# TensorE takes the attention steps of a two-layer hybrid encoder in pairs

## The reference, cut to what matters

```
h   = RMSNorm(x);  q, k, v, g of three mixers = h @ w_in
A   : 12 heads, windowed (+-128 tokens), sink logit, relative bias
B   : 12 heads, dense, normed and rotated q/k
C   : 8 heads, three dilated groups, merged by their softmax denominators
x   = x + concat(A*silu(gA), B*silu(gB), C*silu(gC)) @ w_out
```

## Time and profile before

| | |
|---|---|
| median of 3 runs | 2954.18 us (2950.13 to 2955.64) |
| the profiled execution | 2959.1 us, its span 2957.3 us |
| PE busy | 2899.2 us, 98% of the span |
| DVE, ACT, POOL busy | 1318.9, 1144.8, 921.4 us |
| mean granted TensorE clock | 0.985 of full speed |

### The profile page before, as it was taken

The page is one execution under the profiler, slowest core; times in us unless marked ns, Lnnn a source line. Parts: engine busy times, 40 slices in busy tenths (PEclk is TensorE's granted clock), DMA queues, the critical chain, the costliest instruction groups (busy, mean ns, idle before and its releaser), DMA issues. The chain is left out here.

```text
span 2957.3 us, 43364 instructions
## 1 busy us (share of the span) xinstructions
PE 2899.2 (98%) x15201; PEld 2572.9 (87%) x15201; DVE 1318.9 (45%) x3437; ACT 1144.8 (39%) x2841; POOL 921.4 (31%) x838
## 2 busy tenths in 40 slices
PE   8999999999999999999999999999999999999999
PEld 6888899989999999888888888999899998998887
DVE  3334433325776567522322344333347755774221
ACT  4322223326665466422322322222356644663111
POOL 0233322210663477200002333323006634771000
PEclk9999999998999999999999999999979999999999
DMA  4334333467445332433323343334764453324332
GB/s 165 84 104 111 103 111 100 108 165 200 123 115 129 110 94 72 152 123 102 100 86 91 104 118 107 100 100 109 187 177 106 113 133 99 103 69 164 107 100 93
DMA packets 382034, 342.74 MB, mean 116 GB/s; under 512 B 60055, under 2 KB 310071, under 8 KB 381820
## 3 DMA queue, kind: packets, MB, share of 16 engines
q1 hardware_dynamic: 381820, 339.98, 40.1%
HBM read 256.03 MB, written 83.86 MB: 115 GB/s over the span
## 5 line engine op out<-in xcount | busy, mean ns | idle before, releaser
L1244 PE MATMUL bank<-w_hi,act_hi 128*128 128x512 f32 x2496 | 1001.1, 401 | 4.7 <-DVE w_lo L1667 4.7
L1245 PE MATMUL bank<-w_lo,act_hi 128*128 128x512 f32 x2496 | 989.4, 396 | 0.0
L1246 PE MATMUL bank<-w_hi,act_lo 128*128 128x512 f32 x2496 | 989.1, 396 | 0.0
L1667 DVE TENSOR_TENSOR w_lo<-w_raw,w_hi 128x512 fp32r<-128x512 f32 x544 | 396.2, 730 | 660.9 <-ACT w_hi L1421 659.2
L1421 ACT CAST w_hi<-w_raw 128x512 fp32r<-128x512 f32 x544 | 335.6, 618 | 779.3 <-PE bank L1246 776.9
L1244 PEld LDWEIGHTS bank<-w_hi,act_hi 128*128 128x128 f32 x2496 | 518.2, 208 | 95.8 <-DVE w_lo L1667 5.5
L1246 PEld LDWEIGHTS bank<-w_hi,act_lo 128*128 128x128 f32 x2496 | 518.1, 208 | 95.1
L1245 PEld LDWEIGHTS bank<-w_lo,act_hi 128*128 128x128 f32 x2496 | 518.4, 208 | 88.8
L2024 POOL TENSOR_SCALAR prob<-prob,denom 128x256 f32<-128x256 f32 (+2 forms) x288 | 344.1, 1200 | 322.0 <-DVE denom L1798 321.7
L1267 PE MATMUL bank<-act_hi,w_hi 128*128 128x384 f32 x1024 | 350.4, 342 | 0.0
L1269 PE MATMUL bank<-act_hi,w_lo 128*128 128x384 f32 x1024 | 347.3, 339 | 0.0
(11 more groups left out here) (101 smaller groups left out, 3454.8 us busy)
## 6 DMA issues: line engine op xcount, KB each, us to landing
w_raw<-w_in SPq DMA_DIRECT2D x144, 512.0 KB, 4.1
w_raw<-w_out SPq DMA_DIRECT2D x64, 512.0 KB, 4.4
heads_t<-turned SPq DMA_DIRECT2D x240, 128.0 KB, 2.4
q_t<-heads_t SPq DMA_DIRECT2D x192, 128.0 KB, 2.1
k_t<-keys_t SPq DMA_DIRECT2D x48, 384.0 KB, 5.7
w_raw<-w_in SPq DMA_DIRECT2D x32, 448.0 KB, 3.6
quad_t<-heads_t SPq DMA_DIRECT2D x48, 256.0 KB, 4.8
mix_rows<-mixed_t SPq DMA_DIRECT2D x32, 384.0 KB, 2.7
```

The costliest lines, as they stand in the source:

```text
L1244: pe.matmul(acc[t][:], hi, w_hi[:, n % W_RING, :], start=(k == 0), stop=False)
L1245: pe.matmul(acc[t][:], hi, w_lo[:, n % W_RING, :], start=False, stop=False)
L1246: last = pe.matmul(acc[t][:], lo, w_hi[:, n % W_RING, :], start=False, stop=(k == KC - 1))
L1667: nc.vector.tensor_tensor(w_lo[:, n % W_RING, :], w_raw[:, load % W_RAW, j, :], w_hi[:, n % W_RING, :].bitcast(F32), ALU.subtract).then_in ...
```

## The change

TensorE's list in the loop goes by `PE_TURNS`: the 24 turns of Q one at a time, all later ones in pairs (i, i+1), with i even. For a pair it issues both scores, then the gate pieces of both turns, then what `pair_pv`, the transposes, `pv` and `mix_turn` have for both. The lists of the other engines keep their order turn by turn, as do all lags and the numbers of banks and slots.

Beside it, kind Q's products go to two banks in turn. C's merge is divided: VectorE scales and adds the first three token tiles of the stored parts (`merge_first`), GpSimd the other three (`merge_back`), VectorE's own part comes at turns 6 and 7 after the merge's end where it was 7 and 8, and the transposes at 8 and 10 where they were 9 and 10. `gate_product` works by halves of 384 tokens, one turn apart.

```diff
@@ -307,8 +307,9 @@
 PARTS_TURN = 3
-OWN_TURN = 7
-MIX_TURN = 9
+FRONT_TURN = 4
+OWN_TURN = 6
+MIX_TURNS = (8, 10)
 assert N_PAIRS % STAT_SLOTS == 0 and STAT_SLOTS % TT == 0 and (N_PAIRS - N_MERGES) // 2 % TT == 0
@@ -407,14 +408,26 @@
+def mix_turns(i):
+
+    return [(mc, g) for mc, end in enumerate(MERGE_END) for g, since in enumerate(MIX_TURNS) if i - end == since]
+
+
+
+FIRST_PAIR = next(i for i, x in enumerate(STEPS) if x["kind"] != "Q")
+assert FIRST_PAIR % 2 == N_LOOP % 2 == 0
+PE_TURNS = [(i,) for i in range(FIRST_PAIR)] + [(i, i + 1) for i in range(FIRST_PAIR, N_LOOP, 2)]
+
+
 def bank_users():
     users = []
-    for i in range(N_LOOP):
+    for turns in PE_TURNS:
         for lag, kinds in ((PAIR_LAG, "AB"), (V_LAG, "C")):
-            if 0 <= i - lag < N_STEPS and STEPS[i - lag]["last"] and STEPS[i - lag]["kind"] in kinds:
-                users.append((STEPS[i - lag]["kind"], STEPS[i - lag]["item"]))
-        users += [("mix", (mc, g)) for mc, g in merge_turns(i, MIX_TURN, len(MIX_GROUPS))]
+            for i in turns:
+                if 0 <= i - lag < N_STEPS and STEPS[i - lag]["last"] and STEPS[i - lag]["kind"] in kinds:
+                    users.append((STEPS[i - lag]["kind"], STEPS[i - lag]["item"]))
+        users += [("mix", x) for i in turns for x in mix_turns(i)]
     return users
@@ -471,10 +484,10 @@
 CHUNK_LAST = [max(x["step"] for x in ITEMS if x["kind"] != "Q" and CHUNK_ORDER.index(x["unit"]["chunk"] + x["hp"]) == n) for n in range(KC)]
-PRODUCT_TURN = [max(SILU_TURN[n], CHUNK_LAST[n] + (X_LAG if n in TURNED_CHUNKS else MIX_TURN + len(MIX_GROUPS) - 1)) + 1
+PRODUCT_TURN = [max(SILU_TURN[n], CHUNK_LAST[n] + (X_LAG if n in TURNED_CHUNKS else MIX_TURNS[-1])) + 1
                 for n in range(GATE_TILES)]
-PRODUCT_AT = at_turns(enumerate(PRODUCT_TURN))
-assert all(PRODUCT_TURN[n] < min(i for i, x in GATE_DRAIN_AT.items() if (n + GATE_SLOTS, 0) in x) for n in range(GATE_TILES - GATE_SLOTS))
+PRODUCT_AT = at_turns(((n, h), turn + h) for n, turn in enumerate(PRODUCT_TURN) for h in range(2))
+assert all(PRODUCT_TURN[n] + 1 < min(i for i, x in GATE_DRAIN_AT.items() if (n + GATE_SLOTS, 0) in x) for n in range(GATE_TILES - GATE_SLOTS))
@@ -712,6 +725,7 @@
         merge_parts = sem("merge_parts")
+        merge_front = sem("merge_front")
         kept = sem("kept")
@@ -1036,7 +1050,7 @@
                 at = l * KC + n
-                sp.wait_ge(gated, at + 1)
+                sp.wait_ge(gated, 2 * (at + 1))
                 sp.dma_start(mix_rows[n], mixed_t[:, at % MIX_SLOTS, :]).then_inc(mix_stored[at % MIX_SLOTS], 16)
@@ -1321,9 +1335,10 @@
                 else:
-                    o = o_bank[0]
-                    if it >= 1:
-                        pe.wait_ge(part_taken, l * N_QUADS + ITEMS[it]["quad_no"])
+                    q = ITEMS[it]["quad_no"]
+                    o = o_bank[q % 2]
+                    if q >= 2:
+                        pe.wait_ge(part_taken, l * N_QUADS + q - 1)
                 kv, times = kv_place(l, st["u"])
@@ -1386,20 +1401,25 @@
                 pe.wait_ge(acc_copied, (l + 1) * NS_IN * TT)
-                for i in range(N_LOOP):
-                    first, end = PIECES_BY[i - 1] if i else PIECES_FIRST, PIECES_BY[i]
-                    if i < N_STEPS:
-                        scores(l, i)
-                    for p in range(first, end):
+                for turns in PE_TURNS:
+                    for i in turns:
+                        if i < N_STEPS:
+                            scores(l, i)
+                    first = PIECES_BY[turns[0] - 1] if turns[0] else PIECES_FIRST
+                    for p in range(first, PIECES_BY[turns[-1]]):
                         gate_piece(l, p)
-                    if ends_pair(i - PAIR_LAG):
-                        pair_pv(l, i - PAIR_LAG)
-                    if 0 <= i - T_LAG < N_STEPS:
-                        p_turn(l, i - T_LAG)
-                    if 0 <= i - V_LAG < N_STEPS and not features_first(STEPS[i - V_LAG]):
-                        pv(l, i - V_LAG)
-                    for mc, g in merge_turns(i, MIX_TURN, len(MIX_GROUPS)):
-                        mix_turn(l, mc, g)
+                    for i in turns:
+                        if ends_pair(i - PAIR_LAG):
+                            pair_pv(l, i - PAIR_LAG)
+                    for i in turns:
+                        if 0 <= i - T_LAG < N_STEPS:
+                            p_turn(l, i - T_LAG)
+                    for i in turns:
+                        if 0 <= i - V_LAG < N_STEPS and not features_first(STEPS[i - V_LAG]):
+                            pv(l, i - V_LAG)
+                    for i in turns:
+                        for mc, g in mix_turns(i):
+                            mix_turn(l, mc, g)
@@ -1520,7 +1540,8 @@
                 if ATT_UNITS[u]["kind"] == "B" and ATT_UNITS[u - 1]["kind"] == "C":
-                    act.wait_ge(merge_parts, 3 * (l + 1) * MERGES)
+                    act.wait_ge(merge_parts, 2 * (l + 1) * MERGES)
+                    act.wait_ge(merge_front, 2 * (l + 1) * MERGES)
                 if k > 0:
@@ -1825,7 +1846,7 @@
                 nc.vector.tensor_copy(part_out[:, q % PART_SLOTS, :, 0:2 * DH],
-                                      o_bank[0][:, 0:4 * DH].rearrange("p (h n) -> p h n", h=2)).then_inc(part_taken, 1)
+                                      o_bank[ITEMS[it]["quad_no"] % 2][:, 0:4 * DH].rearrange("p (h n) -> p h n", h=2)).then_inc(part_taken, 1)
@@ -1865,6 +1886,19 @@
+            def merge_first(l, mc):
+
+                m = l * MERGES + mc
+                views = [x[:, 0:TT // 2, :] for x in part_heads]
+                dve.wait_ge(merge_chain, 5 * m + 5)
+                for g in range(2):
+                    v = views[g].rearrange("p t (r d) -> p t r d", d=DH)
+                    w = merge_w[:, g * TT:g * TT + TT // 2, :].unsqueeze(3).broadcast_to([P, TT // 2, 2, DH])
+                    ins = nc.vector.tensor_tensor(v, v, w, ALU.mult)
+                ins.then_inc(merge_front, 1)
+                dve.wait_ge(merge_front, 2 * m + 1)
+                nc.vector.tensor_tensor(views[0], views[0], views[1], ALU.add).then_inc(merge_front, 1)
+
             def merge_own(l, mc, h):
@@ -1875,7 +1909,7 @@
                 dve.wait_ge(merge_scaled, 2 * m + h + 1)
-                dve.wait_ge(merge_parts, 3 * m + 3)
+                dve.wait_ge(merge_parts if h else merge_front, 2 * m + 2)
                 nc.vector.tensor_tensor(own, own, part_heads[0][:, tiles, :], ALU.add).then_inc(merged, 1)
@@ -1884,7 +1918,7 @@
                 if at >= GATE_SLOTS:
-                    dve.wait_ge(gated, at - GATE_SLOTS + 1)
+                    dve.wait_ge(gated, 2 * (at - GATE_SLOTS + 1))
                 tokens = slice(h * HALF, (h + 1) * HALF)
@@ -1949,6 +1983,8 @@
                         merge_weights(l, mc)
+                    for mc, _ in merge_turns(i, FRONT_TURN):
+                        merge_first(l, mc)
                     for mc, h in merge_turns(i, OWN_TURN, 2):
@@ -2033,31 +2069,31 @@
-            def gate_product(l, n):
+            def gate_product(l, n, h):
                 at = l * GATE_TILES + n
-                pool.wait_ge(gate_done, 2 * (at + 1))
+                pool.wait_ge(gate_done, 2 * at + h + 1)
+                tokens = slice(h * HALF, (h + 1) * HALF)
                 if n in TURNED_CHUNKS:
                     pool.wait_ge(mixed, l * N_TURNED + TT * (TURNED_CHUNKS.index(n) + 1))
                 else:
                     pool.wait_ge(mix_copied, (l * MERGES + n + 1 - sum(c < n for c in TURNED_CHUNKS)) * len(MIX_GROUPS))
-                v = mixed_t[:, at % MIX_SLOTS, :]
-                nc.gpsimd.tensor_tensor(v, v, gate_t[:, at % GATE_SLOTS, :], ALU.mult).then_inc(gated, 1)
-
-            def merge_others(l, mc, stage):
+                v = mixed_t[:, at % MIX_SLOTS, tokens]
+                nc.gpsimd.tensor_tensor(v, v, gate_t[:, at % GATE_SLOTS, tokens], ALU.mult).then_inc(gated, 1)
+
+            def merge_back(l, mc, stage):
                 m = l * MERGES + mc
-                pool.wait_ge(merge_chain, 5 * m + 5)
-                if stage < 2:
+                views = [x[:, TT // 2:TT, :] for x in part_heads]
+                if stage == 0:
+                    pool.wait_ge(merge_chain, 5 * m + 5)
                     for g in range(2):
-                        tiles = slice(stage * TT // 2, (stage + 1) * TT // 2)
-                        v = part_heads[g][:, tiles, :].rearrange("p t (r d) -> p t r d", d=DH)
-                        w = merge_w[:, g * TT + stage * TT // 2:g * TT + (stage + 1) * TT // 2, :].unsqueeze(3)
-                        ins = nc.gpsimd.tensor_tensor(v, v, w.broadcast_to([P, TT // 2, 2, DH]), ALU.mult)
+                        v = views[g].rearrange("p t (r d) -> p t r d", d=DH)
+                        w = merge_w[:, g * TT + TT // 2:(g + 1) * TT, :].unsqueeze(3).broadcast_to([P, TT // 2, 2, DH])
```

(14 more changed lines are left out.)

## The result

The changed kernel takes 3315.78 us (median of 4 runs, 3312.74 to 3317.54) against 2953.46 before (median of 4); the ratio is 1.1227, 95% interval 1.1207 to 1.1246. Its profiled span is 3310.9 us, 353.6 more. It is slower by 12.3% where 11.6% was forecast.

A forecast was written before the change was run, and what follows sets the result against it. TensorE's own list was taken to set the pace. Waits 257, splits and drains 70, C's product 5 and clock 61, less gains of 50, gave +343 us and 3297 us against the runs; range 3160 to 3481.

The forecast's parts named there:

- The chain: In A and B pairs, scores wait for copies, exponentials and minimum behind the transposes of i-3: 257 us together.
- Rival 3: Faster: the second step's minimum reaches DVE ahead of the transposes of i-3, nobody waits, 2904 us; chance 0.04.
- The splits: In A and B, 44 odd-turn weight splits between exponential and inversion add 1.25 us each: 55 us.
- The drains: In A and B, 28 even-turn gate drains between low part and inversion add 0.55 us each: 15 us.
- the scores are no trouble: In C, scores were to wait for nothing: DVE has no low part to wait for, two products lie between.
- The product of i-3: In C, this product follows its own transposes in the same pair and waits 0.15 us over 32 pairs: 5 us.
- The clock: Falls of TensorE's clock after waits, taken for three in four of B's 48 four-tile pairs: 61 us.
- The gains: Savings of 50 us in sum, among them 21 of four waits removed and 10 of clock falls after them.
- The 18.5 us for fewer changes between transposes and scores: Gain on TensorE: 0.08 us for 144 pairs, 11.5 us, and in C 0.15 for 48 pairs, 7 us.

The follow-up runs named there:

- e6: The changed kernel with each weight split that falls on an odd turn moved one turn on, 29 a layer: 3217.47 us.
- e3: The changed kernel with the second step's minimum moved ahead of the low part of step i-3 in VectorE's list, TensorE's untouched: 3153.62 us.
- e4: As e3, and on ScalarE both exponentials of a pair also moved ahead of the high copies of i-3 and i-2 respectively: 3060.62 us.
- e2: The changed kernel, pairs kept, with products and transposes ahead of the gate pieces within a pair: 2959.64 us, ratio 1.0014 to before.
- e5: The changed kernel with only the first of a pair's transposes (step i-3) moved ahead of the gate pieces: 3023.73 us.
- e1: The changed kernel with all turns single, its quad banks, divided merge and half products kept: 2924.03 us, ratio 0.9895 to before.

## Why the prediction was right

**The chain.** It holds step by step. To count each wait in full I take from TensorE's timeline the distance between the start of the instruction ahead of the scores and that of the scores, less the same distance where nothing waits. The profile's idle time is shorter, as it begins when the modelled end of the instruction ahead is reached. The first four rows are the usual wait of pairs without a split or drain in the chain, the next two what these add. Changed kernel, us:

| | forecast | measured |
|---|---|---|
| A, second scores, 2 / 3 tiles | 1.31 / a little more | 1.48 / 1.51 |
| B, 4 tiles, first | 1.20 | 1.25 |
| B, 4 tiles, second | 1.13 | 1.06 |
| B, 2 tiles, both together | 2.0 | 2.1 |
| a split on an odd turn adds | 1.25 | 1.1 (A), 1.0 (B), 1.4 (C), by e6 |
| a drain on an even turn adds | 0.55 | 0.2 to 0.3 |
| A, all waits | 132 us | 127 us |
| B, all waits | 195 us | 178 us |
| C, all waits | 0 | 25 us |
| sum | 327 us | 330 us |

e3 and e4 show that the order in DVE's and ACT's lists makes the waits; e2 and e5 show that the transposes' place in TensorE's does; e1 shows that there are none without pairs. Rival 3 named the same point of decision, and the runs put it on the side of the forecast. B's waits are smaller than said: 17 us less in sum, though its usual pair is as forecast.

**The splits.** e6 bears out the term, 1.07 us each by the idle times. The drains were charged at their full 0.55 us and cost about half of that or less. What the prediction missed is C. There it said "the scores are no trouble", because no low part stands ahead of the minimum. But a split does. The pair at 1020 of the changed kernel, on TensorE:

```profile
1020.50 0.36 PE L1310 MATMUL bank<-k_t,q_t 128*128 128x256 f32 x1
...
1022.12 0.39 PE L1310 MATMUL bank<-k_t,q_t 128*128 128x256 f32 x1 [1.14 <-DVE minus_max L1801]
```

On ScalarE:

```profile
1020.26 0.60 ACT L1441 CAST w_hi<-w_raw 128x512 fp32r<-128x512 f32 x1
```

On VectorE:

```profile
1020.90 0.69 DVE L1688 TENSOR_TENSOR w_lo<-w_raw,w_hi 128x512 fp32r<-128x512 f32 x1 [4.24 <-ACT w_hi L1441]
1021.51 0.55 DVE L1801 CUSTOM_DVE_ANT_0 prob<-bank,bias 128x384 f32<-128x384 f32 x1
```

The high part of the weights waits on ScalarE behind the copy of i-3 and the exponential, the low part on VectorE for it, and the minimum of the second step for that. Six of C's pairs a layer wait for such a split (the seventh split stands before a score of B), and three at the start of the stage wait without one while A's last steps are still turned. Together they make 25 us. e6 takes C back to 117.9 us. The product of i-3, priced at 5 us, shows no wait.

**The clock.** Forecast 61 us, all of it in B. By the record of the clock, B stood at 1.2 GHz for 92.2 us in both layers and A for 30.8, which cost at most 46 and 15, 61 in all. The size is right, the place not quite. In A the eight falls all stand at an idle stretch of 1.9 to 3.1 us before the second scores, but A has 24 such stretches, and 16 of them brought no fall. What decides between them stays open. C has one fall, at an idle stretch of 1.32 us. In B, e3 keeps the double waits and 61.4 us at 1.2 GHz in both layers; e4 leaves one wait of 0.7 to 0.8 us a pair, and only 3.4 us in both. The Trainium skill's page TensorE: Matmul & The Clock Gate, section "HAM oscillation — how this bites in real kernels", tells of a kernel in which each pass of the loop starts at the low clock. The trace disagrees for this one: there are 31 low stretches in A and B for 144 pairs.

**The gains.** Forecast were 21 us of waits and 10 of clock, and e1 gains 31.0. The sum is right, its parts are not. The four waits fell from 21.2 to 3.5 us, but that for the copy `prob_t` grew from 5.6 to 10.1, so 13 us are net. The clock gave more than 10: in the profiled executions the time at 1.2 GHz fell from 86.2 to 31.6 us, worth up to 27. By stage of e1 against before the gains lie in Q (19), B (17), A (3) and C (1), in spans, which differ by 38. The 18.5 us for fewer changes between transposes and scores are the term that failed; its step was "The first score matmul after transposes holds the next one off by 0.20, the second by 0.12". It read one row of a pair of rows.

**The sum.** The changed kernel's span is 391 us above that of e1, which has no pairs. Its scores wait 330 us from start to start, e1's 11, and it stands at 1.2 GHz for 140 us more, which costs up to 70. That makes up to 389, so hardly anything is left over. Against the kernel before, whose span is 38 us above e1's, it is 353.6, where 343 were forecast. That the total came so near is in part luck. The forecast left out C's 25 us and counted 18.5 of gain that isn't there. Against that, B's waits were 17 us less than said, A's waits and C's product 5 each, and the other parts gained 38 us of span instead of 31. By stage, A grew by 68 us a layer where 64 was forecast, B by 103 where 126 was.

## What to carry to other kernels

When one engine's list is regrouped, walk the lists of its partners in their own order: anything that stood one turn behind may now stand behind something at the end of the group. Here a chain of copies, exponentials and a minimum of under 3 us was hidden by one spare step. Taking that step cost 12%, though every engine but TensorE had room. A change of the kind of matmul is priced by the whole sequence, start of the group to start of the next, never by the one row that looks long.

## What the runs showed of the hardware

In these traces the last of a group of float32 transposes (128 columns) holds the next matmul off by 0.03 us instead of 0.11, and the matmul behind it holds its successor off by 0.08 more than its like, be it a score (0.20 for 0.12) or a gate matmul (0.26 for 0.17). The total is that of the separate parts. And the granted clock moved with the waits: 0.974 in the mean with 288 us of idle time before the scores, 0.986 with 226, when 58 waits, most of them the long ones, were cut by about 1 us each.
